# Six stationary operands of a transformer kernel at other byte offsets in SBUF, the program otherwise as it was

## The reference

```python
for l in range(DEPTH):                      # first block
    h = rms_norm(x, ffn1_norm[l])
    x = x + FFN_RES_WEIGHT * swiglu(h, ffn1_wg[l], ffn1_wu[l], ffn1_wd[l])
...
    mix = jnp.concatenate([y_ret, y_moba, y_conv], axis=-1)[:, :s]
    x = x + mix @ w_out[l]
...
    x = x + FFN_RES_WEIGHT * swiglu(h, ffn2_wg[l], ffn2_wu[l], ffn2_wd[l])
...
for l in range(L):                          # second block, the inputs that end in _2
...
        h = h + 0.5 * ga1 * _swiglu(n, ffn_w_in[l, 0], ffn_w_out[l, 0])
        h = h + ga2 * _token_mixing(n, ...)
        h = h + 0.5 * ga3 * _swiglu(n, ffn_w_in[l, 1], ffn_w_out[l, 1])
```

## Time and profile before

| | |
|---|---|
| median of 3 runs | 2415.5 us (2412.5 to 2415.85) |
| the profiled execution, its own time | 2414.8 us |
| its span, first to last instruction | 2412.8 us |
| PE busy | 2287.7 us (95%), 10872 instructions |
| DVE busy | 1620.0 us (67%) |
| ACT busy | 1131.1 us (47%) |
| mean granted TensorE clock | 0.981 of full speed |
| DMA | 462.7 MB, 192 GB/s on average |

### The profile page before, as it was taken

How to read it: one execution, slowest core, us unless ns; L and a number is a source line. 1 busy time by engine, 2 the same in 40 slices (tenths; PEclk the granted TensorE clock), 3 DMA queues, 4 the chain that set the end, 5 groups by cost and what they waited for, 6 DMA issues and landing times.

```text
span 2412.8 us, 27143 instructions
## 1 busy us (share of the span) xinstructions
PE 2287.7 (95%) x10872; PEld 1904.2 (79%) x10872; DVE 1620.0 (67%) x2559; ACT 1131.1 (47%) x1707; POOL 19.7 (1%) x26
## 2 busy tenths in 40 slices
PE   7999899999999899989999999899999999998998
PEld 6888678888888778868887877688787778777887
DVE  4556765555557669967985556789689955557565
ACT  4445454444444454444444545444444445554443
POOL 0000000000000000000000000000000000000000
PEclk9999999999999999989999999999999999998999
DMA  7554335555553458847974433588679844335563
GB/s 251 188 187 149 112 124 199 185 192 175 189 186 118 127 167 297 301 168 253 306 266 140 127 116 111 174 281 296 208 275 304 290 138 136 123 100 177 200 212 122
DMA packets 250385, 462.72 MB, mean 192 GB/s; under 512 B 9542, under 2 KB 55536, under 8 KB 250132
## 3 DMA queue, kind: packets, MB, share of 16 engines
q1 hardware_dynamic: 250020, 460.85, 56.8%
q10 hardware_dynamic: 240, 0.16, 0.0%
HBM read 459.92 MB, written 1.05 MB: 191 GB/s over the span
## 4 chain that ended last, share of the span: by engine, by line
PE 68%; DVE 17%; issue 10%; ACT 5%; POOL 0%; DMA 0%; SPq 0%; DVEq 0%; POOLq 0%; ACTq 0%
PE ps L1514 14%; PE ps L1517 14%; PE ps L1515 14%; PE s L1517 5%; PE s L1514 5%; PE s L1515 5%; DVE wl L2003 5%; DVE acc L2011 3%; PE ps L1489 3%; DVE cacc L2197 2%; PE s L1575 1%; ACT wh L1760 1%; PE ps L1595 1%; ACT pt L1824 1%; PE ps L1530 1%
## 5 line engine op out<-in xcount | busy, mean ns | idle before, releaser
L2003 DVE TENSOR_TENSOR wl<-raw,wh 128x1024 fp32r<-128x1024 f32 (+1 forms) x748 | 861.9, 1177 | 331.4 <-ACT wh L1760 325.6
L1760 ACT ACTIVATE wh<-raw 128x1024 fp32r<-128x1024 f32 (+1 forms) x748 | 742.3, 1019 | 345.1 <-PE ps L1517 238.1
L1514 PE MATMUL ps<-wh,xh 128*128 128x512 f32 (+3 forms) x1728 | 674.2, 390 | 18.0 <-DVE wl L2003 11.5
L1515 PE MATMUL ps<-wl,xh 128*128 128x512 f32 (+3 forms) x1728 | 656.3, 380 | 0.0
L1517 PE MATMUL ps<-wh,xl 128*128 128x512 f32 (+3 forms) x1728 | 656.1, 380 | 0.0
L1514 PEld LDWEIGHTS ps<-wh,xh 128*128 128x128 f32 x1728 | 330.8, 191 | 93.9 <-DVE wl L2003 18.0
L1517 PEld LDWEIGHTS ps<-wh,xl 128*128 128x128 f32 x1728 | 330.4, 191 | 53.0
L1515 PEld LDWEIGHTS ps<-wl,xh 128*128 128x128 f32 x1728 | 331.4, 192 | 49.3
L2011 DVE SCALAR_TENSOR_TENSOR acc<-raw,condT,acc 128x512 f32<-128x512 f32 x252 | 189.3, 751 | 7.7
L1514 PE MATMUL s<-wh,xh 128*128 128x512 f32 x384 | 150.2, 391 | 1.8 <-DVE wl L2003 1.8
L1517 PE MATMUL s<-wh,xl 128*128 128x512 f32 x384 | 149.6, 389 | 0.0
(11 more groups left out here) (313 smaller groups left out, 2514.4 us busy)
## 6 DMA issues: line engine op xcount, KB each, us to landing
raw<-in_ffn_w_in SPq DMA_DIRECT2D x80, 1024.0 KB, 5.2
raw<-in_ada_w SPq DMA_DIRECT2D x72, 1024.0 KB, 5.2
raw<-in_ffn_wg SPq DMA_DIRECT2D x40, 1024.0 KB, 5.2
raw<-in_ffn_wu SPq DMA_DIRECT2D x40, 1024.0 KB, 5.2
raw<-in_ffn_wd SPq DMA_DIRECT2D x40, 1024.0 KB, 5.1
raw<-in_ffn_w_out SPq DMA_DIRECT2D x40, 1024.0 KB, 5.2
raw<-in_mix_w_in SPq DMA_DIRECT2D x28, 1024.0 KB, 5.1
raw<-in_w_in SPq DMA_DIRECT2D x28, 768.0 KB, 4.4
```

The lines of the kernel that those rows point to most:

```text
L1514: e.matmul(o, X[0](kk, t), hi, start=kk == 0, stop=False)
L1515: e.matmul(o, X[0](kk, t), lo, start=False, stop=False)
L1760: ins = self.e.activation(m.wh[j % NH][:, 0:n], m.raw[u % NR][:, k0 * w:k0 * w + n], ACT.Copy)
L2003: ins = self.e.tensor_tensor(m.wl[j % NH][:, 0:n], m.raw[u % NR][:, k0 * w:k0 * w + n], hi, ALU.subtract)
```

## The change

It moves six buffers. hTh begins 16 bytes later (4 floats) and hTl 256 bytes; yh 8 bytes and yl 128; y1h 48 bytes (12 floats) and y1l 64. xh and xl, all weight buffers and the layout before hTh stay. The upper buffers are made by the new `past`: it allocates a row that is 16 floats longer and returns a view that begins n floats into it. Since hTh and hTl end 512 bytes later, sg, hb, vT, junk, dg, acc, ach, acl and the rows of the set-up move by 512 bytes and keep their phase. On every engine the instructions, their order and their waits are the same as before; only addresses differ.

```diff
-        self.hTh = sb("hTh", [P, 22, S], F32R)
-        self.hTl = sb("hTl", [P, 22, S], F32R)
+        self.hTh = self.past("hTh", 22, u0, 4)
+        self.hTl = at("hTl", [P, 22, S], F32R, u0 + 22 * 1024 + 256)
+        self.top = u0 + 44 * 1024 + 512
...
-        self.yh = at("yh", [P, 8, S], F32R, u0)
-        self.yl = at("yl", [P, 8, S], F32R, u0 + 8192)
+        self.yh = self.past("yh", 8, u0, 2)
+        self.yl = at("yl", [P, 8, S], F32R, u0 + 8192 + 128)
...
-        self.y1h = at("y1h", [P, 8, S], F32R, self.top)
-        self.y1l = at("y1l", [P, 8, S], F32R, self.top + 8192)
+        self.y1h = self.past("y1h", 8, self.top, 12)
+        self.y1l = at("y1l", [P, 8, S], F32R, self.top + 8192 + 64)
...
+    def past(self, name, nk, at, n):
+
+        t = self.at(name, [P, nk * S + 16], F32R, at)
+        return t[:, n:n + nk * S].rearrange("p (k s) -> p k s", s=S)
```

## The result

The changed kernel takes 2420.7 us in the median of 8 runs (2417.9 to 2426.1), the kernel before 2413.7 us beside it (2412.5 to 2415.9). The ratio is 1.0028, with a 95% interval of 1.0018 to 1.0039: slower by 7.0 us, or 0.28%. The time lies within the range of the forecast, but I had forecast no change, and there is one that is clear of its interval. The profiled run of the changed kernel is the slowest of its 8: 2426.1 us of its own, a span of 2424.1, at a mean granted clock of 0.978; the other seven have 0.980 to 0.982.

The account below looks back on a forecast made before the run. TensorE, busy for 95% of the span, was taken as the bound. All parts summed to 0 on the profiled 2414.8 us; with the runs' median 0.7 above that sum, the forecast was 2415.3 us, range 2405 to 2426.

Parts of the forecast that it names:

- What bounds the kernel, and the count: TensorE, busy 95% of the span; 2496 matmuls get a moved stationary operand, a nanosecond on each being 2.5 us.
- I take the 390-column row: 390-column chunk, second K tile 24 bytes off phase: 178 ns on or off, so 0 ns extra for a moved phase.
- (a): Down projections, hTh moved by 16 bytes, 1408 matmuls: 0 us, between -17 and +13 us.
- the slope: Matmul distance by columns, 384 against 512: 0.42 ns a column, giving 175.8 ns for 390 columns.
- The onesr row: adaLN sums' reduction, onesr 320 bytes off phase: matmuls last 9 and 3 ns more; kept as upper end, +9 ns.
- Rival two: Down projection, being in phase is the good case: slower, 9 ns giving 2438 us or 3 ns 2423; chance 0.15.
- (b): Down projections, hTl moved by 256 bytes, 704 matmuls: 0 us, between -8 and +6.
- (c) and (d): Output projections, yh and yl, then y1h and y1l moved: together 384 matmuls, 0 us, between -4.6 and +3.5.
- (e), (f) and (g): ScalarE's and VectorE's writes; everything behind hTl moving 512 bytes; no instruction, wait or DMA added, removed or moved: 0.
- Rival one: Affected matmuls: in-phase reads clash and cost the 12 ns, so offsets give 2385 us, or 2398 to 2407; faster 0.17.
- the 12 ns: Part of every 227 ns matmul distance that does not depend on columns; at most 30 us to gain over 2496 matmuls.
- What would show it: Signs in the rows: if right, hTh and hTl medians stay 389 and down-projection distances 227 ns; xh groups unmoved.

## Why the prediction was wrong

**What bounds the kernel, and the count,** held: 2112 + 384 matmuls, each nanosecond of theirs 2.5 us of the kernel, and the control without a change. 3.7 ns on 2112 make 7.8 us, and 1.9 ns was the bound from which it shows.

**The step that failed** is "I take the 390-column row", which put the term (a), hTh by 16 bytes, at 0; it measured +6.2 us alone. I read 178 ns on phase and 178 ns off phase as "a moved phase costs nothing". But the on-phase side was not a settled row. Its five distances are the first after an interruption: the chunk's first matmul starts at 1371.26 us and the second 282 ns later. The 384-column chunk at 228 us, all on phase, shows what such a start takes: its first five distances after the interruption take 0.89 us, the same as at 390 columns, and the next five 0.87 us, the settled 173 ns each (four lines lie between each pair). First the start of the 390-column chunk, then the 384-column one:

```profile
1371.26 0.44 PE L1514 MATMUL ps<-wh,xh 128*128 128x390 f32 x1
1371.54 0.34 PE L1515 MATMUL ps<-wl,xh 128*128 128x390 f32 x1
```
```profile
228.85 0.34 PE L1515 MATMUL ps<-wl,xh 128*128 128x384 f32 x1
...
229.74 0.33 PE L1514 MATMUL ps<-wh,xh 128*128 128x384 f32 x1
...
230.61 0.33 PE L1517 MATMUL ps<-wh,xl 128*128 128x384 f32 x1
```

So I compared the slow start of a row with its later, off-phase part, and the two came out alike. Besides, the chunk's two K tiles alternate, six matmuls on phase and six off, too few for a rhythm to settle. The sign was in my own sum: both were 2 ns above what the slope gives for 390 columns. On the on-phase side the start of the row explains it. That on the other side it is the cost of the phase fits, but is only argued; no run moved that tile alone.

**The onesr row, which I set aside,** pointed the right way. Its offset of 320 bytes is 64 modulo the 256 that proved harmless, and both at 64 bytes give 6 ns a matmul; that the excess of this short pair has the same cause was not tested. Rival two was right in its mechanism (being in phase is the good case) and in its place, and its medians of 392 to 398 came. Its smaller price, 3 ns on each matmul and 7.5 us, 2423, came close (3.7 ns and 7.0 us, 2420.7) by luck: the 3.7 is no price that each matmul pays, but a mean of rows at 227 and rows at 233, and how many run at 233 nothing in the trace before could tell. I gave it 0.15. The 9 ns of its upper end, 22 us, came out nowhere; the worst mean was 6 ns.

**(a) and (b)**: hTh by 16 bytes is +6.2 us alone, in the bounds of -17 to +13, and hTl by 256 is 0 alone. I named "an effect of 2 ns or more at 16 or 256 bytes that the 24 bytes of the 390-column tile don't show" as what would make me wrong; it was the 16.

**(c) and (d)** held for the time (+0.6 us, within noise) and not for the rows, with about 3 ns a matmul. Whether the 8 bytes of yh cost anything on their own stays open; 16, 32, 64 and 128 bytes cost although each is a whole number of 16 bytes. That the median of y1h, 397 in the kernel before, is none of the phase held: it is the same in the run with all on phase. Its rows are mostly short. The first, from 326.2 us on, has 12 matmuls, whose distances vary between 224 and 236 ns and come down to 227 only at the end, so it never gets past its start.

**(e), (f) and (g)** held: VectorE's and ScalarE's writes are 592 and 685 ns as before, and the run with the neighbours moved shows no change.

**Rival one** is borne out by no run: no offset brought the mean distance of a long 512-column row below 227 ns. Where the 12 ns come from stays open.

**What would show it**: "a price of hTl should appear in the distance behind the wl matmul" was wrong in kind. With hTh alone off phase the three distances of the triple grow alike.

The rule of read ports that take nothing from each other (the Trainium skill, TensorE: Matmul & The Clock Gate, Part 2, step 1), by which, as I wrote, no address matters, does not carry that far here: the same two reads cost +13.7 us at one relation and +0.7, within noise, at another. Whether they meet at a port or behind it these runs do not show.

## What to carry to other kernels

Where a stationary operand is loaded under every matmul, lay it out so that its start and that of the weights that stream meanwhile differ by nothing, 256 or 512 bytes (these were free; 16 to 128 cost up to 6 ns of 227 a matmul at 512 columns). A time per instruction that is steady over a hundred of them can be one of several: look at the minimum beside the median, and at a long row of starts, and compare long rows with long rows. A comparison inside the first dozen matmuls after an interruption can't show what a rhythm costs. Where medians of a few runs differ by some us, look at the granted clock of each run before ranking them; the distances from start to start at full clock are the better measure of a price of a few ns.

## What the runs showed of the hardware that I had not expected

Back-to-back matmuls of 512 float32r columns, each with its own stationary operand, run at 227 ns when the two operands are on phase, in the down projections after a start of up to ten uneven distances (224 to 236 ns). With hTh 16 bytes off they run at 227 or at 233 ns, with xh 16 bytes off also at 229. They hold what they took for over a hundred matmuls, with one exception in the run of hTh alone, and take it in other down projections from one kernel to the next. With both operands at 32 and 64 bytes off the 227 ns are gone, and the rhythm is 233; at 128 the distances spread from 228 to 241 ns with a mean of 233. With the weights moved by 64 bytes instead, most rows run at 229. What the loads and the stream contend for, and what sets the rhythm where a row starts, these runs do not show.
